# The front of a decoder block on one core, in two halves of the model width

## The chip, the cores and the metric

The kernel runs on one core of a Trainium2 chip. The metric is the device time of one execution in microseconds (us). Its engines are called TensorE (PE in the profile, its weight loads PEld), VectorE (DVE), ScalarE (ACT), GpSimd (POOL) and SyncE (SP, which here only issues DMAs). Each works through its own list of instructions in order and waits on semaphores for the others.

## What is computed

One layer with a sequence of 1024 tokens and model width 1024, in float32. The part that the change touches is its beginning:

```python
mod = (silu(c) @ w_ada + b_ada)[:, None, :]
sh1, sc1, g1, sh2, sc2, g2 = split(mod, 6)          # each of width 1024
h = rms_norm(x, norm1_g) * (1.0 + sc1) + sh1
proj = h @ w_in                                     # q 512 | k 128 | v 128 | u 512
```

After it come sliding-window attention over q, k, v (window 128, rotary positions, sinks), a pooling mixer over u, the projection with `w_o` gated by g1, and an MLP over h2 = RMSNorm(x) * (1 + sc2) + sh2, gated by g2.

## The kernel before

Tokens are handled in eight tiles of 128 (t = 0 to 7), the model width in eight chunks of 128 (k = 0 to 7, `KD` = 8, `P` = 128). Every engine's order is written out by hand.

**Loads.** SyncE walks the list `stream`. Its first 28 entries go round a ring of 12 buffers (four `raw`, eight `slots`): eight pieces of sh1's weights, eight of sc1's, four of `wu` (two chunks of the u weights each), eight of `wqkv` (one chunk of the q, k, v weights each). A piece of sh1 or sc1 holds one k row per partition and all 1024 columns, 512 KB. The load of entry n first waits (`freed`) until entry n - 12 has been used. x of tiles 0 and 1 is loaded behind the eighth entry (`load_x`); x of tile 2 behind the last of the 28, and it waits for the low half of h of tile 0 (`h_lo`), whose buffer it takes. The parameters and the next modulation pieces follow on the same queue.

**Modulation.** VectorE multiplies each piece with its column of `silu` and adds it (`add_piece`) into `acc` for sh1 and `acc_sc` for sc1, so that the sum over the partitions is still to be made. TensorE turns the 128x128 blocks of these sums (`turn_sums`), and VectorE reduces over the turned columns to `b1` (L1219) and to `a1` (`scale_1`, L1226), adds the bias from `cols` and, for `a1`, multiplies with norm1_g. `a1` and `b1` hold one scalar per model column.

**x.** ScalarE squares x (`square_x`), GpSimd makes the root (`root`, L1823 and L1825) behind the constants that it builds from the start (masks and pooling bands, L1767 to L1815), ScalarE scales (`scale_x`, L709), TensorE turns the tile (`turn_x`). VectorE (`make_h`, L1240) or ScalarE (`make_h_half`, L718) then makes h with `a1` and `b1`, a half of the model width at a time.

**High and low parts.** Products are made from numbers split in two: ScalarE copies the high part (`hi_h`, `hi_wu`, `hi_wqkv`), VectorE subtracts it to get the low part (`lo_h` L1246, `lo_wu` L1253, `lo_wqkv` L1259), and TensorE makes three products for each pair (`three`, L1969 to L1971), 512 columns wide for q and u and 256 for k and v. `project` loops over the eight chunks k into one PSUM bank.

**TensorE's order at the front.** Sums of sh1 turned; `keep_clock(8)`, which multiplies the identity with itself; x of tiles 0 and 1 turned; six more; the two halves of sc1's sums turned; `keep_clock(14)`; then u, q and kv of tile 0, u of tile 1, the pooling windows of tile 0 (`pool_windows`, L2095), x of tile 2 turned, q of tile 1, and so on.

The rows name lines; L1965 is the transpose helper `tr`, L1982 is `keep_clock`, L1166 the add of a piece and L1164 the first multiply, L1206 the two half-width adds of the last sc1 piece, L529 and L539 to L543 the loads of x and of the parameters.

Of the kernel before, what the change touches and what calls it, by code (L numbers as in the profile page):

```python
# [16 lines left out]
P = 128  # L17
# [36 lines left out]
def build(nc, x, c, positions, w_ada, b_ada, norm1_g, w_in, q_norm_g, k_norm_g, attn_sinks,  # L54
# [30 lines left out]
    with ExitStack() as ctx:  # L85
# [133 lines left out]
        stream = [("sh1", k) for k in range(KD)]  # L219
        stream += [("sc1", k) for k in range(KD)]  # L220
        stream += [("wu", k) for k in range(KD // 2)]
        stream += [("wqkv", k) for k in range(KD)]
# [11 lines left out]
        WO_POOL, WO_DVE = (0, 5, 6), (1, 2, 3, 4, 7)  # L234
        JOB_LOADS = (4, 4, 4, 3, 4, 4, 1, 0)
# [33 lines left out]
        sc1_turned = sem("sc1_turned")  # L269
# [56 lines left out]
        def rq(t):  # L326
            return rqs[:, NHD_ROOTS * (t % 3):NHD_ROOTS * (t % 3) + NHD_ROOTS]

# [139 lines left out]
        def freed(eng, n):  # L468
# [5 lines left out]
            if kind in ("sh1", "sc1"):  # L474

                eng.wait_ge(mod_summed, k + 1 + (KD if kind == "sc1" else 0) + (kind == "sc1" and k == KD - 1))
# [9 lines left out]
        def source(kind, k):  # L486
# [10 lines left out]
            m = mod_of[kind]  # L497
            return wada[:, k, m * D:(m + 1) * D]

        def target(kind, a):  # L500
            if kind == "wu":
# [18 lines left out]
        def _(sp):  # L520
# [5 lines left out]
            def load_x(t):  # L526
                if t >= 2:
                    sp.wait_ge(h_lo, 2 * (t - 1))
# [4 lines left out]
            for n in range(first_job):  # L533
                load(n)
                if n == 7:
# [155 lines left out]
        def _(act):  # L691
# [20 lines left out]
            def make_h_half(t):  # L712

                if t == 0:
                    act.wait_ge(a1_ready, 2)
                act.wait_ge(x_turned, t + 1)
                for k in range(NK, KD):
                    ins = nc.scalar.activation(xh[:, t % 2, k * P:(k + 1) * P], xT_banks(t)[:, k * P:(k + 1) * P],  # L718
                                               ACT.Identity, bias=b1[:, k:k + 1], scale=a1[:, k:k + 1])
                ins.then_inc(h_half[1], 1)  # L720
# [34 lines left out]
            hi_wqkv(6)  # L755
            hi_wqkv(7)
            hi_h(1, 1)
# [64 lines left out]
            def keep_u(t):  # L822
# [3 lines left out]
                nc.scalar.copy(usb[:, t % 2, :], bank(0)).then_inc(u_kept, 1)  # L826
# [322 lines left out]
        def _(dve):  # L1149
# [45 lines left out]
            for n in range(2 * KD):  # L1195
                if n >= 1:
                    dve.wait_ge(mod_summed, n)
                if n < KD:
                    add_piece(acc[:, :], ("sh1", n), n, mod_summed)
                elif n < 2 * KD - 1:  # L1200
                    add_piece(acc_sc, ("sc1", n - KD), n - KD, mod_summed)
                else:
                    a = landed(dve, ("sc1", KD - 1))
                    for h in range(2):
                        cut = slice(512 * h, 512 * h + 512)
                        v.scalar_tensor_tensor(out=acc_sc[:, cut], in0=a[:, cut], scalar=silu[:, KD - 1:KD],  # L1206
                                               in1=acc_sc[:, cut], op0=ALU.mult, op1=ALU.add).then_inc(mod_summed, 1)
                if n == 4:
                    dve.wait_ge(rows_in, 16 * 4)
                    v.tensor_copy(rows[64:72, :], posi[64:72, :]).then_inc(posf_ready, 1)  # L1210
                if n == KD + 2:

                    dve.wait_ge(rows_turned, 1)
                    v.tensor_copy(cols[:, :], psum[:, 4, 0:72]).then_inc(cols_ready, 1)
                if n == 2 * KD - 4:

                    dve.wait_ge(cols_ready, 1)
                    dve.wait_ge(mod_turned, 1)
# [1187 lines left out]
```

## Time and profile before

| what | value |
|---|---|
| median of 3 runs | 964.57 us (964.04 to 966.05) |
| profiled execution, its own time | 966.11 us |
| its span, first to last instruction | 964.4 us |
| granted TensorE clock, mean | 1.0 |
| TensorE busy | 925.0 us, 96% |
| VectorE busy | 657.4 us, 68% |
| ScalarE busy | 492.3 us, 51% |
| GpSimd busy | 352.6 us, 37% |

Times in the rows are counted from the start of the span of one profiled execution. The span lies 1.7 us below that execution's own time. A matmul's own duration overlaps with that of the next, so the pace of a series is read from start to start.

### The profile page before, as it was taken

The page shows a single profiled execution, that of the slowest core. Times are in us where ns is not written, and L with a number is a line of the kernel's source. Part 1 is how long each engine was busy: PE and PEld are TensorE (multiplying, and loading weights), DVE is VectorE, ACT ScalarE, POOL GpSimd, SP SyncE. Part 2 cuts the span into 40 slices and gives each one's busy share as a digit, 9 for nine tenths or more (in the row PEclk, how much of TensorE's full clock was granted, in tenths as well). Part 3 has the DMA queues.
Part 4 walks back from the last instruction along what each step waited for, and adds up shares of the span by engine and source line. Part 5 has one row for each costly group of instructions (what it writes and reads, how often), then busy time and mean ns, then how long its engine had stood idle before and what let it go on. Part 6 is the DMA issues. An engine that isn't in the chain of part 4 may idle for free.

```text
span 964.4 us, 12633 instructions
## 1 busy us (share of the span) xinstructions
PE 925.0 (96%) x4411; PEld 765.2 (79%) x4411; DVE 657.4 (68%) x1000; ACT 492.3 (51%) x874; POOL 352.6 (37%) x342
## 2 busy tenths in 40 slices
PE   1898999998999999999999999999999999999998
PEld 1787788886778888787888788888888888888887
DVE  6876887878644687665556544535786666779896
ACT  1656777778464564644554455454443444333331
POOL 8032222215232443988888877851000000000000
DMA  9852332214222240665456533538999637987673
GB/s 360 298 170 93 131 110 79 78 64 153 89 88 87 88 154 22 222 213 176 154 169 210 177 132 133 173 138 276 351 345 333 226 99 239 308 307 245 227 252 113
DMA packets 92271, 175.54 MB, mean 182 GB/s; under 512 B 9320, under 2 KB 26288, under 8 KB 92208
## 3 DMA queue, kind: packets, MB, share of 16 engines
q1 hardware_dynamic: 92096, 174.70, 53.1%
q8 instruction: 35, 0.57, 0.2%
q14 instruction: 28, 0.23, 0.1%
q10 hardware_dynamic: 112, 0.04, 0.0%
HBM read 136.95 MB, written 37.75 MB: 181 GB/s over the span
## 4 chain that ended last, share of the span: by engine, by line
PE 84%; DVE 6%; ACT 5%; POOL 3%; issue 2%; DVEq 0%; POOLq 0%; ACTq 0%
PE psum L1969 26%; PE psum L1971 25%; PE psum L1970 25%; PE psum L1965 3%; ACT probs L780 2%; PE psum L2045 1%; PE psum L2068 1%; ACT probs L788 1%; POOL band L1788 1%; PE psum L2095 1%; PE psum L2026 1%; PE psum L2023 1%; PE psum L2024 1%; ACT qT L799 1%; DVE probs L1297 1%
## 5 line engine op out<-in xcount | busy, mean ns | idle before, releaser
L1076 ACT CAST down_operands<-down_raw 128x1024 fp32r<-128x1024 f32 x96 | 100.9, 1054 | 153.4 <-PE psum L1971 58.1
L1969 PE MATMUL psum<-down_operands 128*128 128x512 f32 x448 | 174.3, 389 | 0.0
L1970 PE MATMUL psum<-down_operands 128*128 128x512 f32 x448 | 174.3, 389 | 0.0
L1971 PE MATMUL psum<-down_operands 128*128 128x512 f32 x448 | 174.3, 389 | 0.0
L1705 DVE TENSOR_TENSOR down_operands<-down_raw,down_operands 128x1024 fp32r<-128x1024 f32 x93 | 112.5, 1219 | 19.1 <-ACT down_operands L1076 18.5
L1969 PE MATMUL psum<-h2T,w_operands 128*128 128x512 f32 x272 | 107.5, 395 | 1.9 <-DVE act_quads_a L1649 1.3
L1971 PE MATMUL psum<-h2T,w_operands 128*128 128x512 f32 x272 | 105.9, 390 | 0.0
L1970 PE MATMUL psum<-h2T,w_operands 128*128 128x512 f32 x272 | 105.9, 389 | 0.0
L1921 POOL TENSOR_TENSOR w_operands<-raw,w_operands 128x512 fp32r<-128x512 f32 x56 | 83.2, 1487 | 42.1 <-ACT w_operands L1028 42.1
L1969 PEld LDWEIGHTS psum<-down_operands 128*128 128x128 f32 x448 | 84.1, 188 | 17.6
L1970 PEld LDWEIGHTS psum<-down_operands 128*128 128x128 f32 x448 | 84.1, 188 | 17.4
L1971 PEld LDWEIGHTS psum<-down_operands 128*128 128x128 f32 x448 | 84.1, 188 | 17.3
L1823 POOL TENSOR_SCALAR small<-small 128x1 f32<-128x1 f32 (+2 forms) x23 | 8.3, 359 | 169.1 <-DVE small L1366 131.7
L1971 PE MATMUL psum<-t_sums_hi,w_operands 128*128 128x512 f32 x168 | 65.4, 389 | 0.0
L1969 PE MATMUL psum<-t_sums_hi,w_operands 128*128 128x512 f32 x168 | 65.4, 389 | 0.0
L1970 PE MATMUL psum<-t_sums_lo,w_operands 128*128 128x512 f32 x168 | 65.4, 389 | 0.0
L1969 PE MATMUL psum<-w_in_hi,hT_hi 128*128 128x512 f32 (+1 forms) x168 | 61.7, 368 | 2.7 <-DVE hT_lo L1246 1.7
L1969 PEld LDWEIGHTS psum<-h2T,w_operands 128*128 128x128 f32 x272 | 51.1, 188 | 15.8 <-issue 3.8
L1921 POOL TENSOR_TENSOR w_operands<-w_sums,w_operands 128x512 fp32r<-128x512 f32 x42 | 55.9, 1343 | 11.8 <-ACT w_operands L1028 11.8
L1970 PEld LDWEIGHTS psum<-h2T,w_operands 128*128 128x128 f32 x272 | 51.1, 188 | 10.8 <-issue 0.5
L1971 PE MATMUL psum<-w_in_hi,hT_lo 128*128 128x512 f32 (+1 forms) x168 | 59.6, 355 | 0.0
L1971 PEld LDWEIGHTS psum<-h2T,w_operands 128*128 128x128 f32 x272 | 51.1, 188 | 10.7
(251 smaller groups left out, 1973.4 us busy)
## 6 DMA issues: line engine op xcount, KB each, us to landing
down_raw<-in_w_mlp_out SPq DMA_DIRECT2D x160, 256.0 KB, 4.3
down_raw<-act_scratch SPq DMA_DIRECT2D x112, 256.0 KB, 3.3
raw<-in_w_ada SPq DMA_DIRECT2D x32, 512.0 KB, 4.7
raw<-in_w_mlp_in SPq DMA_DIRECT2D x32, 512.0 KB, 4.9
act_scratch<-act_quads_a SPq DMA_DIRECT2D x64, 256.0 KB, 2.2
act_scratch<-act_quads_b SPq DMA_DIRECT2D x48, 256.0 KB, 3.6
slots<-in_w_ada SPq DMA_DIRECT2D x8, 512.0 KB, 10.5
xh<-in_x SPq DMA_DIRECT2D x8, 512.0 KB, 6.1
```

What stands on the lines that cost most here:

```text
L780: nc.scalar.activation(pr[:, kv, h, 0:w], pr[:, kv, h, 0:w], ACT.Exp, bias=negm[:, hh:hh + 1], scale=rq(i)[:, hh:hh + 1], accum_out=den[:, ...
L788: ins = nc.scalar.activation(pr[:, kv, h, 0:w], pr[:, kv, h, 0:w], ACT.Copy, scale=rden[:, kv * G + h:kv * G + h + 1])
L799: nc.scalar.copy(qT[r, :, :].rearrange("p (m e) q -> p m e q", e=2)[:, :, e, :], bank(1)[r, :].rearrange("p (m q) -> p m q", q=P))
L1076: nc.scalar.copy(o[:, 0, :, :], r[:, 0:2, :]).then_inc(op2_hi, 1)
L1297: ins = v.tensor_tensor_reduce(out=pr[:, kv, h, 0:w], in0=banks(4)[:, 256 * h:256 * h + w], in1=mask[:, m0:m0 + w], scale=1.0, scalar=-3e3 ...
L1705: v.tensor_tensor(o[:, 1, :, :], r[:, 0:2, :], f32(o[:, 0, :, :]), ALU.subtract).then_inc(op2_lo_dve, 1)
L1788: own_p.step(g.affine_select(out=cut, in_=cut, compare_op=ALU.is_ge, fill=0.0, base=base, pattern=[[1, n]], channel_multiplier=-1))
L1921: g.tensor_tensor(o[:, 1, :, :], quad, o[:, 0, :, :].bitcast(F32), ALU.subtract).then_inc(w1_lo, 1)
L1965: return nc.tensor.transpose(o, i, ident[0:rows_, 0:rows_])
L1969: mm(o, wh, ah, start=first, stop=False, skip_group_check=adds)
L1970: mm(o, wh, al, start=False, stop=False, skip_group_check=adds)
L1971: return mm(o, wl, ah, start=False, stop=last, skip_group_check=adds)
```

## The change

The two modulations sh1 and sc1 are made in two halves of 512 columns. A piece holds 512 columns of two k rows per partition (still 512 KB), and `stream` has sh1, sc1, wu and wqkv of the first half (4, 4, 2 and 4 pieces) and then those of the second. x of tiles 0 and 1 is loaded behind the fourth piece. VectorE adds each piece in two half-width instructions (`add_half`). Piece 4 of sh1 and of sc1 is not added by VectorE; TensorE multiplies it with `silu` straight into the column sums (`sum_piece`). The turning and reducing of the sums is replaced by matmuls with a column of ones (`sum_columns`, an output one column wide per block), and VectorE adds the bias from PSUM (`shift_1`, `scale_1`). The products of tile 0 and the u products of tile 1 are made for chunks 0 to 3 first and for chunks 4 to 7 later into the same banks (`project_half`); u of tile 1 has bank 4 to itself. h of tile 1 is made by ScalarE alone (`make_h_act`), h of tile 0 in its first half by VectorE and in its second by ScalarE. The first halves of h of both tiles come ahead of the second halves, which `h_count` counts. The sines of ScalarE move behind the pooled copy of tile 0, the root of x of tile 2 on GpSimd ahead of the root of q and k of tile 0. Counts of `mod_turned` and `mod_taken` drop by one throughout.

```diff
+        for h in range(2):
+            stream += [("sh1", 4 * h + j) for j in range(4)]
+            stream += [("sc1", 4 * h + j) for j in range(4)]
+            stream += [("wu", 2 * h + j) for j in range(2)]
+            stream += [("wqkv", 4 * h + j) for j in range(4)]
...
+        PE_PIECE = 4
...
+        def h_count(t, h):
+            return (2 * h + t if t < 2 else 2 * t + h) + 1
...
+            if kind in ("sh1", "sc1"):
+                at = m * D + 512 * (k // 4)
+                return wada[:, 2 * (k % 4):2 * (k % 4) + 2, at:at + 512]
...
                 if t >= 2:
-                    sp.wait_ge(h_lo, 2 * (t - 1))
+                    sp.wait_ge(h_lo, h_count(t - 2, 1))
...
-                if n == 7:
+                if n == 3:
                     load_x(0)
                     load_x(1)
```

ScalarE:

```diff
             hi_wu(0)
+            hi_h(0, 0)
             hi_wu(1)
-            hi_h(0, 0)
-            make_h_half(0)
-            hi_h(0, 1)
+            hi_wqkv(0)
+            hi_wqkv(1)
+            make_h_act(1, 0)
+            hi_h(1, 0)
+            hi_wqkv(2)
+            hi_wqkv(3)
             hi_wu(2)
             hi_wu(3)
-            for k in range(5):
-                hi_wqkv(k)
-            make_h_half(1)
+            hi_wqkv(4)
             hi_wqkv(5)
-            hi_h(1, 0)
+            for t in range(2):
+                make_h_act(t, 1)
+                hi_h(t, 1)
             hi_wqkv(6)
             hi_wqkv(7)
-            hi_h(1, 1)
...
-            sines()
             scale_x(2)
             keep_u(1)
             keep_pooled(0)
+            sines()
```

VectorE (the new list is whole from the first piece on):

```diff
+            def add_half(kind, k):
+                nonlocal summed
+                h, a = k // 4, landed(dve, (kind, k))
+                to = (acc if kind == "sh1" else acc_sc)[:, 512 * h:512 * h + 512]
+                for j in range(2):
+                    c_ = 2 * (k % 4) + j
+                    if summed >= 1:
+                        dve.wait_ge(mod_summed, summed)
+                    if j == 0 and k in (0, PE_PIECE + 1):
+                        v.tensor_scalar(to, a[:, 0:512], silu[:, c_:c_ + 1], None, ALU.mult).then_inc(mod_summed, 1)
+                    else:
+                        v.scalar_tensor_tensor(out=to, in0=a[:, 512 * j:512 * j + 512], scalar=silu[:, c_:c_ + 1],
+                                               in1=to, op0=ALU.mult, op1=ALU.add).then_inc(mod_summed, 1)
+                    summed += 1
...
+            for k in range(4):
+                add_half("sh1", k)
+            add_half("sc1", 0)
...
+            add_half("sc1", 1)
+            add_half("sc1", 2)
...
+            add_half("sc1", 3)
+            dve.wait_ge(cols_ready, 1)
+            shift_1(0)
             scale_1(0)
             make_h(0, 0)
-            scale_1(1)
             lo_wu(0)
             lo_h(0, 0)
             lo_wu(1)
+            lo_wqkv(0)
+            lo_wqkv(1)
+            lo_h(1, 0)
+            add_half("sh1", 5)
+            lo_wqkv(2)
+            lo_wqkv(3)
+            add_half("sh1", 6)
+            add_half("sh1", 7)
+            for k in range(PE_PIECE + 1, KD):
+                add_half("sc1", k)
+            lo_wu(2)
+            shift_1(1)
+            scale_1(1)
+            lo_wu(3)
             lo_h(0, 1)
-            lo_wu(2)
-            lo_wu(3)
-            for k in range(4):
-                lo_wqkv(k)
-            make_h(1, 0)
-            for k in range(4, KD):
-                lo_wqkv(k)
-            lo_h(1, 0)
+            lo_wqkv(4)
+            lo_wqkv(5)
             lo_h(1, 1)
+            lo_wqkv(6)
+            lo_wqkv(7)
```

TensorE (`column_sum` is one fp32 matmul with one moving column):

```diff
+            def sum_columns(at, sums, h):
+                for n in range(4 * h, 4 * h + 4):
+                    ins = column_sum(at, n, sums[:, n * P:(n + 1) * P], ones[:, 0:1], h == 0, True)
+                ins.then_inc(cols_summed, 1)
+            def sum_piece(at, kind):
+                a = landed(pe, (kind, PE_PIECE))
+                for j in range(2):
+                    for n in range(4):
+                        ins = column_sum(at, 4 + n, a[:, 512 * j + n * P:512 * j + (n + 1) * P], silu[:, j:j + 1],
+                                         j == 0 and n == 0, False)
+                ins.then_inc(piece_used, 1)
+            pe.wait_ge(mod_summed, 8)
+            sum_columns(1, acc, 0)
             pe.wait_ge(posf_ready, 1)
             tr(psum[:, 4, 0:72], rows[0:72, :], 72).then_inc(rows_turned, 1)
...
-            keep_clock(8, 2)
+            keep_clock(2, 2)
             turn_x(0)
             pe.wait_ge(cols_ready, 1)
             turn_x(1)
-            keep_clock(6, 2)
...
+            pe.wait_ge(mod_summed, 16)
+            sum_columns(2, acc_sc, 0)
             keep_clock(14, 0)
-            project_u(0)
-            project(bank(6), 0, AW, 0).then_inc(q_done, 1)
-            project(psum[:, 3, 0:2 * KVW], AW, QKV, 0).then_inc(kv_done, 1)
-            project_u(1)
+            project_half(bank(0), QKV, IN, 0, 0, u=True)
+            sum_piece(1, "sh1")
+            project_half(bank(6), 0, AW, 0, 0)
+            project_half(psum[:, 3, 0:2 * KVW], AW, QKV, 0, 0)
+            project_half(u_bank(1), QKV, IN, 1, 0, u=True)
+            pe.wait_ge(mod_summed, mod_count("sh1", KD - 1))
+            sum_columns(1, acc, 1)
+            sum_piece(2, "sc1")
+            pe.wait_ge(mod_summed, mod_count("sc1", KD - 1))
+            sum_columns(2, acc_sc, 1)
+            pe.wait_ge(b1_ready, 2)
+            keep_clock(12, 1)
+            project_half(bank(0), QKV, IN, 0, 1, u=True).then_inc(u_done, 1)
+            project_half(bank(6), 0, AW, 0, 1).then_inc(q_done, 1)
+            project_half(psum[:, 3, 0:2 * KVW], AW, QKV, 0, 1).then_inc(kv_done, 1)
+            project_half(u_bank(1), QKV, IN, 1, 1, u=True).then_inc(u_done, 1)
             pool_windows(0)
+            pe.wait_ge(u_kept, 2)
             turn_x(2)
```

## Rows read from the trace of the kernel before

**Rows 1.** The page: busy time, share of the span and instructions of each engine.

```profile
PE 925.0 (96%) x4411; PEld 765.2 (79%) x4411; DVE 657.4 (68%) x1000; ACT 492.3 (51%) x874; POOL 352.6 (37%) x342
```

**Rows 2.** Busy time by stretch: length, then each engine's, clock, DMA share, GB/s.

```profile
0.00:38.00 38.00, 15.56 (x90) 14.51 (x90) 27.91 (x38) 10.45 (x16) 22.28 (x70) 1.00 0.97 373
```

**Rows 3.** Timeline of TensorE: start, duration, what, count, idle before and its releaser.

```profile
22.38 3.78 PE L1982 MATMUL psum<-ident 128*128 128x128 f32 x16 [4.08 <-DVE squares L1166]
26.80 3.68 PE L1965 MATMUL psum<-ident,xh 128*128 128x128 f32 x16 [0.64 <-ACT xh L709]
...
32.94 3.29 PE L1982 MATMUL psum<-ident 128*128 128x128 f32 x28
37.97 0.50 PE L1969 MATMUL psum<-w_in_hi,hT_hi 128*128 128x512 f32 x1 [1.75 <-DVE hT_lo L1246]
...
51.00 0.28 PE L1969 MATMUL psum<-w_in_hi,hT_hi 128*128 128x256 f32 x1
...
53.86 0.40 PE L1969 MATMUL psum<-w_in_hi,hT_second 128*128 128x512 f32 x1
...
59.33 1.14 PE L2095 MATMUL psum<-band,u_rows 128*128 128x144 f32 x8
```

**Rows 4.** Timeline of VectorE, first piece to last low part.

```profile
5.21 0.75 DVE L1164 TENSOR_SCALAR acc<-raw,small 128x1024 f32<-128x1024 f32 x1 [1.07 <-DMA raw<-in_w_ada]
...
12.34 3.93 DVE L1166 SCALAR_TENSOR_TENSOR acc<-slots,small,acc 128x1024 f32<-128x1024 f32 x3
18.11 0.75 DVE L1164 TENSOR_SCALAR squares<-slots,small 128x1024 f32<-128x1024 f32 x1 [1.84 <-DMA slots<-in_w_ada]
...
24.89 1.22 DVE L1219 TENSOR_REDUCE small<-psum 128x8 f32<-128x1024 f32 x1
...
28.87 1.42 DVE L1206 SCALAR_TENSOR_TENSOR squares<-raw,small,squares 128x512 f32<-128x512 f32 x2
32.70 0.69 DVE L1226 TENSOR_REDUCE small<-psum 128x4 f32<-128x512 f32 x1 [2.42 <-PE psum L1965]
...
33.82 1.36 DVE L1240 TENSOR_SCALAR xh<-psum,small 128x128 f32<-128x128 f32 x4
...
36.09 1.22 DVE L1253 TENSOR_TENSOR w_in_lo<-slots,w_in_hi 128x1024 fp32r<-128x1024 f32 x1
37.23 0.68 DVE L1246 TENSOR_TENSOR hT_lo<-xh,hT_hi 128x512 fp32r<-128x512 f32 x1
...
46.60 3.55 DVE L1259 TENSOR_TENSOR w_in_lo<-raw,w_in_hi 128x768 fp32r<-128x768 f32 x4
```

**Rows 5.** Timeline of GpSimd in the first 26 us.

```profile
8.36 1.30 POOL L1796 TENSOR_TENSOR band<-band,ident 128x128 f32<-128x128 f32 x1
...
17.10 0.20 POOL L1791 TENSOR_SCALAR_AFFINE_SELECT band<-band 128x16 f32<-128x16 f32 x1
...
23.79 1.77 POOL L1825 TENSOR_TENSOR small<-small 128x2 f32<-128x2 f32 x1
```

**Rows 6.** Timeline of ScalarE from the scaling of x on.

```profile
25.59 2.19 ACT L709 ACTIVATE xh<-xh,small 128x1024 f32<-128x1024 f32 x2 [7.68 <-POOL small L1825]
28.74 1.05 ACT L733 CAST w_in_hi<-slots 128x1024 fp32r<-128x1024 f32 x1 [0.96 <-DMA slots<-in_w_in]
...
35.22 0.62 ACT L728 CAST hT_hi<-xh 128x512 fp32r<-128x512 f32 x1 [4.07 <-DVE xh L1240]
36.21 1.51 ACT L718 ACTIVATE xh<-psum,small 128x128 f32<-128x128 f32 x4 [0.37 <-DVE small L1231]
...
40.17 3.03 ACT L737 CAST w_in_hi<-slots 128x768 fp32r<-128x768 f32 x4
```

**Rows 7.** Timeline of SyncE's DMA issues: x of tile 2 and the last parameter.

```profile
39.68 0.33 SPq L529 DMA_DIRECT2D xh<-in_x  x1
...
42.59 0.43 SPq L543 DMA_DIRECT2D small<-in_attn_sinks  x1
```

**Rows 8.** DMA issues of the first 60 us: KB each, median us to landing.

```profile
small<-in_attn_sinks SPq DMA_DIRECT2D x1, 4.0 KB, 5.5
```

More of the change, by code:

```diff
@@ L215, in banks @@
             return psum[:, j:j + 2, :].rearrange("p b n -> p (b n)")
[L219 to L222, printed above, removed]
+        stream = []
+        for h in range(2):
[3 more added lines that the diff above has]
+            stream += [("wqkv", 4 * h + j) for j in range(4)]
         EARLY = len(stream)
@@ L234, in build @@
         WO_POOL, WO_DVE = (0, 5, 6), (1, 2, 3, 4, 7)
+        PE_PIECE = 4
+        DVE_PIECES = [(kind, 4 * h + j) for h in range(2) for kind in ("sh1", "sc1") for j in range(4) if 4 * h + j != PE_PIECE]
         JOB_LOADS = (4, 4, 4, 3, 4, 4, 1, 0)
@@ L474, in freed @@
             if kind in ("sh1", "sc1"):
-                eng.wait_ge(mod_summed, k + 1 + (KD if kind == "sc1" else 0) + (kind == "sc1" and k == KD - 1))
+                if k == PE_PIECE:
+                    eng.wait_ge(piece_used, 1 + (kind == "sc1"))
+                else:
+                    eng.wait_ge(mod_summed, mod_count(kind, k))
             elif kind in adaln_jobs:
@@ L497, in source @@
             m = mod_of[kind]
+            if kind in ("sh1", "sc1"):
+                at = m * D + 512 * (k // 4)
+                return wada[:, 2 * (k % 4):2 * (k % 4) + 2, at:at + 512]
             return wada[:, k, m * D:(m + 1) * D]
         def target(kind, a):
-            if kind == "wu":
+            if kind in ("wu", "sh1", "sc1"):
                 return a.rearrange("p (k n) -> p k n", k=2)
@@ L1193, in angles @@
                 v.tensor_scalar(a1_, a3, -1.0, float(np.pi / 2), ALU.mult, ALU.add).then_inc(angles_ready, 1)
[L1195 to L1218, printed above, removed]
-                    v.tensor_reduce(b1, banks(0).rearrange("p (k n) -> p k n", n=P), AX_X, ALU.add).then_inc(mod_taken, 1)
-                    dve.wait_ge(mod_taken, 1)
-                    own_d.step(v.tensor_tensor(b1, b1, cols[:, 8 * SH1:8 * SH1 + 8], ALU.add))
@@ L1988, in turn_sums, with project_half @@
                 return ins
-            def project(o, a, b, t, u=False):
-                for k in range(KD):
+            def project_half(o, a, b, t, half, u=False):
+                for k in range(4 * half, 4 * half + 4):
                     if u and k % 4 == 0:
-                        pe.wait_ge(h_lo, 2 * t + k // 4 + 1)
+                        pe.wait_ge(h_lo, h_count(t, half))
                     if t == 0 and u:
@@ L1999, in project @@
                     ins = three(o, h[:, k, :], l[:, k, :], wih[:, k, a:b], wil[:, k, a:b], k == 0, k == KD - 1)
+                return ins
+            def project(o, a, b, t, u=False):
+                for h in range(2):
+                    ins = project_half(o, a, b, t, h, u)
                 return ins
@@ L2101, in _, with column_sum @@
             pe.wait_ge(rows_in, 16 * 4)
+            def column_sum(at, n, a, by, first, last):
+                return mm(psum[:, at, n:n + 1], a, by, start=first, stop=last, skip_group_check=True)
+            def sum_columns(at, sums, h):
[11 more added lines that the diff above has]
+            sum_columns(1, acc, 0)
             pe.wait_ge(posf_ready, 1)
             tr(psum[:, 4, 0:72], rows[0:72, :], 72).then_inc(rows_turned, 1)
-            pe.wait_ge(mod_summed, KD)
-            turn_sums(banks(0), acc).then_inc(mod_turned, 1)
-            pe.wait_ge(mod_summed, 2 * KD - 5)
-            keep_clock(8, 2)
+            keep_clock(2, 2)
             turn_x(0)
```

73 lines of the change are left out of this document (41 added, 32 removed).

## The prediction

> **What bounds the kernel now.** The busy times come first: TensorE works 925.0 of 964.4 us [rows 1], so any time that is to be won lies where TensorE stands. The row of the first 38 us holds most of its 39 us of idle time: it works 15.56 us there, while the DMA engines are 0.97 busy at 373 GB/s [rows 2], and so 909.5 of the 926.4 us behind them. The front is the place. Its end I call the mark: the moment at which the products of tile 0 and the u products of tile 1 are done and the pooling windows start, 59.33 us [rows 3]. What TensorE does from the mark on is nearly the same list in both kernels, and nothing in it waits for an absolute time, so I take a shift of the mark as a shift of the end and look afterwards for what could eat it.
>
> Then the order of time on each engine. TensorE starts its first product at 37.97 us, released by VectorE's low part of h; 24 products of 512 columns take 59.33 - 53.86 = 5.47 us (0.228 each) and 24 of 256 columns 2.86 us (0.119 each) [rows 3]. VectorE is occupied from 5.21 us, when the first piece of the modulation has landed, to about 50.1 us, the end of its last low part of the q, k, v weights [rows 4]. The eleventh transfer (eight pieces and two tiles of x are ahead of or equal to it) is what VectorE waits for at 18.11 us, so one transfer of 512 KB costs (18.11 - 5.21)/10 = 1.29 us [rows 4]. TensorE still has some 9 us of products at 50.1 us. So before, VectorE's list sets the mark, and the transfers set only its first third.
>
> **Transfers.** The same bytes are loaded in another order. In 1.29 us steps the eight half-width pieces of the first half and the two tiles of x are there at 5.21 + 9 x 1.29 = 16.8 us, the last piece of the second half (eight more pieces, two of wu, four of wqkv at three quarters) at about 33.5 us, the last wqkv near 40 us. Rows of 2 KB instead of 4 KB could cost up to 5% by my estimate; 0.6 us at the first half, and it is covered in both halves, as follows.
>
> **First half on VectorE.** A full add is 3.93/3 = 1.31 us with its wait, a half one 1.42/2 = 0.71 without, 0.78 with it; the full first multiply is 0.75, a half one 0.48 by my estimate (half of what is over a fixed 0.2) [rows 4]. Four pieces of sh1 end at 11.1 us, VectorE waits for sc1 until 13.0, and the fourth sc1 piece is added by about 19.5 us. The reduces over turned sums (1.22 and twice 0.69 us [rows 4]) go; TensorE's column sums replace them.
>
> **What the first half then waits for.** In the changed list of TensorE the sums of sc1's columns stand behind both turns of x, and these stand behind the scaling of x, whose roots GpSimd makes after its constants. That root ends at 23.79 + 1.77 = 25.56 us before [rows 5], where it cost little. Now it is on the path. Does it come sooner? GpSimd's operation with SBUF inputs lasts 1.30 us beside VectorE's adds and a like small select 0.20 us while VectorE idles [rows 5]; each ends just after a VectorE instruction ends. With halves these ends come every 0.78 us. I went through GpSimd's 21 such operations from 5.3 us on: eight pass by 11.2 us, four in the gap to 13.0, seven by 19.4, and the last two (0.2 and 0.55 us) freely: the root is ready at 20.3 us. Bounds: 14.5 us if no operation were held up (they sum to 9 us), 25.6 us if nothing changes.
>
> From the root: ScalarE scales two tiles in 2.19 us [rows 6], TensorE starts 1.2 us after the first and turns both in 3.68 us [rows 3], so it is through at 25.2 us. Eight instructions with one column follow (an fp32 product is two). The trace shows none with one column. Not below 0.05 us each (half of a fast 128-column one, 3.29/28 = 0.117), not above 3.78/16 = 0.236, the slow 128-column one [rows 3]; I take 0.12, 1.0 us. With 0.2 of hand-over and two small VectorE operations (0.43 between the end of the second reduce and the first h, 33.39 to 33.82 [rows 4]) the first four scale columns are ready at about 27.0 us. VectorE has idled 7 us: that is the price of the change.
>
> **VectorE to the second half.** Its list: h of tile 0 1.36, low parts of two wu at 1.14, of four wqkv at 3.55/4 = 0.89, of two halves of h at 0.68, six pieces of modulation (two first multiplies, ten adds: 8.8 us), another wu 1.14 [rows 4]. That is 1.36 + 2.28 + 3.56 + 1.36 + 8.8 + 1.14 = 18.5 us, and 0.7 us of waiting for ScalarE, whose list from the first h (0.62 + 1.05 + 2 x 0.76 + 1.51 + 0.62 [rows 6]) ends as late. The sums end at 45.1, the wu at 46.2; TensorE's eight one-column instructions end at 46.2. The second scale columns are there at 46.8 us. ScalarE makes h (1.51) and its high part (0.62) [rows 6], VectorE the low part (0.68), with hand-overs 3.0 us: the second half of the products starts at 49.8 us. All transfers are over by then, and the loads are issued in time: the latest, of wqkv 4, is freed by a low part at about 37 us. The columns that VectorE saved (piece 4 of both, two reduces, h of tile 1) are 2 x 1.31 + 2.6 + 1.36 = 6.6 us; the idle 7 us and 0.14 us more for each of some dozen split adds eat them.
>
> **TensorE.** First half: free at 26.3 us, 28 instructions to hold the clock, then 12 products of u, eight column pairs, 12 and 12 of q and kv (held by the low parts until 37.5 us), 12 of u for tile 1, and the sums. This ends at about 44.8 us, just before VectorE's 45.1: little is spare. Second half: 36 x 0.228 + 12 x 0.119 = 9.6 us from 49.8 us; the low parts of wqkv come at 50.7, 51.5, 53.1, 54.0 us and are not late. The mark: **59.5 us, 0.2 later than before**.
>
> **Behind the mark.** x(2) and the parameters are issued when the low half of h for tile 0 is there: at 39.68 us before, the last of them at 42.59 [rows 7], with 5.5 us to landing [rows 8]. Now this is at 49.9 us, the last issue at 52.8, landing at 58.3 at the latest. VectorE's gain and sums of q, angles and h of tile 2 wait for it, up to 2.5 us later against the mark than before; TensorE's q of tile 1 needs the gain at mark + 1.8 and gets it at mark + 0.2. Were that cover gone, it would cost that same 2 us. The new wait of the third turn for the kept u is ended while the windows run (1.14 us); behind it stand only that turn and q of tile 1: 0.1 us. The sines move behind the pooled copy, and their user at mark + 11 us has room. Sum: +0.3 us.
>
> **Rivals.** (a) The clock, slower. TensorE's 128-column instructions went at 0.236 us from 22.38 until at least 30.5 us and at 0.117 from 32.94 on [rows 3]: the 1.2 and the 2.4 GHz level. The new list has a stretch of one-column instructions and waits from 42.6 to 46.2 us, ahead of the 24 that hold the clock. If the level falls there, these take 5.7 instead of 2.8 us, 2.2 more than the 3.5 us of h that cover them, and if the slow stretch lasts 8.1 us as the first one did, 2.4 us of the products run at half rate, which loses 1.2: the mark 3.6 later than before, 968.3 us. Against it: 1.7 us of idling ahead of 37.97 did no harm. It decides from a gap that lowers the level at all. (b) The first 28 holding instructions, which now follow 16 turned blocks and eight one-column instructions, all run slow, 6.6 us; TensorE starts its products at 33 us and is about 1.5 us late at the sums: 966.4 us. In my sum a good part of them is fast. For it: the 16 turns at 26.80 us ran at 0.23 us each though 16 holding instructions stood ahead of them [rows 3]. The Trainium skill (TensorE: Matmul & The Clock Gate, part on transposes) says that transposes do not count as work for the clock; the trace agrees as far as those 16 were slow, and by that rule (b) would be the outcome. (c) Faster: GpSimd's chain is held up less than I count; each microsecond off the root is one off the mark until TensorE's list, with its 0.3 us spare, is itself moved with it. A root at 17 us gives -3, 961.6 us. (d) VectorE is not the bound at all: then the last sc1 piece (33.5 us) sets the second half, behind wqkv 5 on ScalarE: products from 41.7 us, mark 51.4 us, 956.7 us. Its list speaks against it. (e) The change does nothing to the root: it stays at 25.6, everything 5.3 later, 970.2 us.
>
> **Numbers.** The profiled execution took 966.11 us with a span of 964.4; the median of the runs is 964.57. A shift of 0.3 us makes 964.9 us. What a measurement of this kernel can tell from no change is about 0.2%, 1.9 us. Chances: my sum within its own errors (one-column price -0.6 to +1.0 at two places, root 0.7, downstream 0.7) 0.38, range 963 to 966.7; (b) 0.10; (a) 0.20; (c) 0.19; (d) 0.06; (e) 0.07. Faster is (c) and (d), 0.25 in all; within 0.2% my sum and half of (b), 0.43; slower the rest, 0.32. The range from 960.5 to 969.3 us leaves out (d), (e) and tails.
>
> **What would show it.** Right: VectorE idle between about 19.5 and 26 us, ended by TensorE; GpSimd's root of the first tiles near 20.3 us; turns of x ending near 25.2; second-half products from about 50 us; windows at 59.5. Wrong: keep-clock instructions at 0.236 us behind 46 us; a root at 17 or 25; waits of TensorE for low parts of wqkv in the second half; VectorE waiting for the parameters so long that q of tile 1 waits too.

## The result and the profile after

The changed kernel takes 967.15 us (median of 16 runs, 966.01 to 968.56), the one before 964.84 (16 runs beside it, 964.04 to 966.52): 1.0022 times as long, 95% interval 1.0015 to 1.0028. The profiled execution has a span of 966.8 us (own time 968.56), 2.4 more than before. The page's busy row, and the stretch that answers to [rows 2] (length, each engine's busy time, clock, DMA share, GB/s):

```profile
PE 932.9 (96%) x4459; PEld 774.8 (80%) x4459; DVE 652.6 (68%) x1005; ACT 494.1 (51%) x878; POOL 349.6 (36%) x342
```

```profile
0.00:38.00 38.00, 20.12 (x104) 18.84 (x105) 24.00 (x41) 14.09 (x21) 16.53 (x70) 1.00 0.96 349
```

By 38 us TensorE has been busy 4.6 us longer than before, and the kernel is not faster: the work came sooner and its end did not. TensorE's timeline, which answers to [rows 3]:

```profile
21.04 3.67 PE L2006 MATMUL psum<-ident,xh 128*128 128x128 f32 x16 [4.12 <-ACT xh L731]
24.51 1.70 PE L2152 MATMUL psum<-ones,squares 128*128 128x1 f32 x8
26.08 5.23 PE L2023 MATMUL psum<-ident 128*128 128x128 f32 x28
31.07 0.48 PE L2010 MATMUL psum<-w_in_hi,hT_hi 128*128 128x512 f32 x1
33.88 1.84 PE L2152 MATMUL psum<-small,raw 128*128 128x1 f32 x16
...
43.44 1.93 PE L2152 MATMUL psum<-small,slots 128*128 128x1 f32 x16
45.23 1.03 PE L2152 MATMUL psum<-ones,squares 128*128 128x1 f32 x8
46.29 4.57 PE L2023 MATMUL psum<-ident 128*128 128x128 f32 x24
50.62 0.48 PE L2010 MATMUL psum<-w_in_hi,hT_hi 128*128 128x512 f32 x1
...
60.34 1.14 PE L2143 MATMUL psum<-band,u_rows 128*128 128x144 f32 x8
```

VectorE's and GpSimd's timelines, which answer to [rows 4] and [rows 5]:

```profile
5.39 0.49 DVE L1231 TENSOR_SCALAR acc<-raw,small 128x512 f32<-128x512 f32 x1 [1.99 <-DMA raw<-in_w_ada]
5.91 2.40 DVE L1233 SCALAR_TENSOR_TENSOR acc<-raw,small,acc 128x512 f32<-128x512 f32 x3
...
26.32 0.16 DVE L1249 TENSOR_TENSOR small<-psum,cols 128x4 f32<-128x4 f32 x1 [5.64 <-PE psum L2152]
...
40.99 4.04 DVE L1233 SCALAR_TENSOR_TENSOR squares<-slots,small,squares 128x512 f32<-128x512 f32 x5
...
46.56 0.16 DVE L1252 SCALAR_TENSOR_TENSOR small<-small,cols 128x4 f32<-128x4 f32 x1
...
48.95 0.69 DVE L1267 TENSOR_TENSOR hT_lo<-xh,hT_hi 128x512 fp32r<-128x512 f32 x1 [1.08 <-ACT hT_hi L749]
...
58.41 0.17 DVE L1432 TENSOR_SCALAR small<-small 128x8 f32<-128x8 f32 x1 [4.69 <-DMA small<-in_attn_sinks]
```

```profile
7.75 0.87 POOL L1838 TENSOR_TENSOR band<-band,ident 128x128 f32<-128x128 f32 x1
...
18.29 0.71 POOL L1865 TENSOR_SCALAR small<-small 128x2 f32<-128x2 f32 x1
19.09 0.72 POOL L1867 TENSOR_TENSOR small<-small 128x2 f32<-128x2 f32 x1
```

How to read them. The root is ready at 19.81 us, VectorE stands still for 5.64 us until the first scale columns come (26.32), its sums end at 45.03, and the low part of h for the second half is ready at 49.64. The row to stop at is TensorE's 46.29: 24 instructions that hold the clock in 4.57 us, 0.19 each, where the 28 of [rows 3] took 0.117 each. The first product behind them starts at 50.62, 0.98 us after h is ready. The windows by stretch (length, TensorE's busy time with its count, clock, DMA share, GB/s) say why, and show a second such place:

```profile
46.00:47.00 1.00, 0.96 (x9) 1.00 0.00 0
47.00:50.00 3.00, 3.00 (x17) 0.51 0.00 0
50.00:51.00 1.00, 1.00 (x8) 0.76 0.45 66
...
228.00:231.00 3.00, 3.00 (x8) 0.50 0.71 232
231.00:235.00 4.00, 4.00 (x24) 0.95 0.68 202
```

From 47 to about 50.4 us and from 228 to 231.3 us TensorE was granted 0.50, the 1.2 GHz level, while it was busy all the time. Before, no profiled stretch behind the start has that. (At the start of both kernels 128-column instructions go at 0.23 us each, the pace of the lower level, and yet the windows give 1.00 there; for the first 30 us the level is read from the pace.)

**Where the 2.4 us are.** The mark moves from 59.33 to 60.34 us, and the windows of tile 7 start at 221.30 instead of 220.22: 1.0 us from the front, nothing lost in the 160 us behind it. From the mark to the end of the span are 905.1 us before and 906.5 after. In ten of the twelve experiments below it is 904.9 to 905.5, and 906.3 in the other two: e9, which has the stretch at 228 us too, and e1, which has a wait behind the mark. So the rest, 1.3 us, is that stretch. TensorE waits 1.11 us there ahead of the pooling products and 0.72 ahead of the first products with w_o, but it does so in the kernel before and in e3 as well, where the level stays up. So the list of instructions and its waits do not bring it on by themselves.

Each run also gives its mean granted clock. A stretch of 3.4 us at half rate takes 3.4 x 0.5 / 965 = 0.002 off that mean. The kernel before had 1.0 in 23 of 28 runs of one batch. The changed one had it in none: 0.998, one stretch, in nine of 16 (median 966.79 us), 0.994 to 0.996 in seven (968.33). That is two such stretches or more, or one twice as long: the profile here has two with 0.996, and that of e7 below has one of 6.8 us with the same 0.996. The runs of the kernel before fall in two groups of their own, near 964.5 and 966.2 us, both at clock 1.0; its profile (966.11) is of the upper one. No profile of the lower one was taken, so what parts them stays open, and differences between profiles and between medians can differ by up to 1.7 us for that reason alone. One run of e8, 1176 us at a mean clock of 0.757, is left out below.

### The profile page after: what moved, and what is told of

Same layout as the page of the kernel before. It is cut to its first block, busy times and chain, and to the rows that moved or that the text cites. A ratio compares the mean times of both kernels' runs of the same rounds, so it can differ in the third digit from the quotient of the medians.

```text
span 966.8 us, 12740 instructions
## 1 busy us (share of the span) xinstructions
PE 932.9 (96%) x4459; PEld 774.8 (80%) x4459; DVE 652.6 (68%) x1005; ACT 494.1 (51%) x878; POOL 349.6 (36%) x342
## 4 chain that ended last, share of the span: by engine, by line
PE 86%; DVE 5%; ACT 5%; POOL 2%; issue 2%; DVEq 0%; POOLq 0%; ACTq 0%
PE psum L2010 26%; PE psum L2012 26%; PE psum L2011 26%; PE psum L2006 3%; ACT probs L804 2%; PE psum L2023 1%; PE psum L2093 1%; PE psum L2116 1%; ACT probs L812 1%; PE psum L2152 1%; PE psum L2143 1%; PE psum L2074 1%; PE psum L2072 1%; PE psum L2071 1%; ACT qT L823 1%
## 5 line engine op out<-in xcount | busy, mean ns | idle before, releaser
L1962 POOL TENSOR_TENSOR w_operands<-raw,w_operands 128x512 fp32r<-128x512 f32 x56 | 83.2, 1486 | 42.2 <-ACT w_operands L1052 42.2
```

Of the source, the lines that this page charges most:

```text
L1962: g.tensor_tensor(o[:, 1, :, :], quad, o[:, 0, :, :].bitcast(F32), ALU.subtract).then_inc(w1_lo, 1)
```

## The experiments

"Mark" is the start of the pooling windows; since the first load lands between 4.9 and 5.5 us in different profiles, the second number is the mark less VectorE's first piece. Even so it is not exact: in the seven profiles whose lists are the same up to the first scale columns (changed, e1, e3, e5, e7, e8, e9) these columns come 19.50 to 20.93 us behind the first piece, and the changed kernel's profile is the latest. So a difference of a microsecond in the mark says nothing unless rows show where it arises. Ratios are to the kernel before on the same chip (whose medians there were 964.65 to 966.18, since they fall in one or the other of its two groups); they are not quotients of two medians.

| kernel | mark / from first piece | slow stretch in the front | span | median, ratio (95%) |
|---|---|---|---|---|
| before | 59.33 / 54.12 | none | 964.4 | 964.84 |
| changed | 60.34 / 54.95 | 47 to 50.4 | 966.8 | 967.15, 1.0022 (1.0015 to 1.0028) |
| e1_sums_earlier | 58.71 / 53.60 | 34.7 to 38.2 | 965.0 | 970.05, 1.0045 (1.0030 to 1.0059) |
| e2_root_earlier | 56.69 / 51.21 | 40.6 to 47.4 | 961.8 | 963.59, 0.9985 (0.9977 to 0.9994) |
| e3_less_adds | 58.29 / 52.99 | 45.0 to 48.4 | 963.8 | 965.95, 1.0012 (1.0001 to 1.0022) |
| e5_no_hold | 60.83 / 55.61 | 46.5 to 53.3 | 966.1 | 967.49, 1.0022 (1.0013 to 1.0031) |
| e7_params_first | 59.87 / 54.81 | 43.6 to 50.4 | 964.9 | 966.91, 1.0019 (1.0010 to 1.0028) |
| e8_sums_params | 61.71 / 56.26 | 35.4 to 42.2 | 966.7 | 968.9, 1.0035 (1.0022 to 1.0049) |
| e9_spread_params | 60.18 / 54.80 | 46.6 to 50.0 | 966.5 | 966.05, 1.0006 (0.9997 to 1.0015) |
| e10_root_spread_params | 56.20 / 51.00 | none | 961.3 | 963.03, 0.9970 (0.9958 to 0.9982) |
| e4_root_earlier_old | 56.97 / 51.82 | none | 962.0 | 963.83, 0.9990 (0.9981 to 0.9998) |
| e11_short_hold | 55.77 / 50.46 | 23.4 to 30.2 | 960.7 | 962.73, 0.9974 (0.9963 to 0.9984) |
| e12_old_colsums | 59.26 / 54.38 | none | 964.3 | 966.04, 1.0011 (1.0000 to 1.0023) |
| e13_old_root_colsums | 55.41 / 50.33 | none | 960.5 | 962.92, 0.9973 (0.9964 to 0.9982) |

### The terms of the changed kernel

**The one-column instructions of sc1 moved away from the holding series.**

```diff
             sum_piece(1, "sh1")
+            sum_piece(2, "sc1")
...
             sum_columns(1, acc, 1)
-            sum_piece(2, "sc1")
```

> The 16 one-column products of sc1's fourth piece move ahead of q of tile 0, so that one-column work ahead of the second holding series is 1.9 us instead of 3.7. Theory (the clock falls because of the one-column stretch, and the slow holding series is what moved the mark): the 24 holding instructions take 2.8 us instead of 4.57, the second half starts at 49.7 instead of 50.62, the windows at 59.4 instead of 60.34; the whole about 1 us below the changed kernel, 966.2. Rival (the level falls at a moment of its own, whatever stands there): the slow stretch stays near 47 us and the windows at 60.3.

TensorE's timeline and windows of it:

```profile
31.56 1.84 PE L2152 MATMUL psum<-small,raw 128*128 128x1 f32 x16
33.26 2.21 PE L2152 MATMUL psum<-small,slots 128*128 128x1 f32 x16
...
45.39 2.92 PE L2023 MATMUL psum<-ident 128*128 128x128 f32 x24
48.96 0.50 PE L2010 MATMUL psum<-w_in_hi,hT_hi 128*128 128x512 f32 x1 [0.65 <-DVE hT_lo L1267]
...
79.29 1.16 PE L2116 MATMUL psum<-pooledT,pool_w 128*128 128x128 f32 x8 [1.34 <-DVE pooledT L1390]
```

```profile
35.00:38.00 3.00, 3.00 (x9) 0.50 1.04 386
```

The holding series is fast again (2.92 us) and TensorE now waits 0.65 us for h, so the 0.98 us were the clock's. The slow stretch did not go: it begins at 34.7 us in the last of the joined 32 one-column instructions and slows the products of q behind them instead. Of the 1.35 us by which the mark is nearer to the first piece, 0.88 was there already at the first scale columns, ahead of the edit. It came out slower: 970.05 us, and the row of 79.29 shows a new wait of 1.34 us behind the mark. Its profile was its lowest run (966.77, clock 0.998); the five others, at 0.993 to 0.995, had more of such stretches, at places that no profile shows.

**The root ahead of the last pooling band.** `root` of x of tiles 0 and 1 is moved on GpSimd ahead of the constants of the last window.

```diff
             for i, w in enumerate(POOL_WINDOWS):
+                if i == 3:
+                    pool.wait_ge(x_squared, 2)
+                    root(rx[:, 0:2], ssx[:, 0:2], D, x_root)
```

> GpSimd makes the root of x of tiles 0 and 1 ahead of its last pooling band. Theory (the root is on the path of the changed kernel): scaling starts at 15.4 us instead of 19.84, the sums of sc1's columns end at 22 instead of 26.2, VectorE's idle time in front of them falls from 5.6 to about 1.5 us, the windows start 2 to 3.9 us earlier (56.4 to 58.3; the smaller gain if TensorE's holding series stays at the slow level), the whole 963 to 965. Rival (TensorE's or the transfers' time sets the second half): the windows move by less than 0.5 us.

ScalarE's timeline:

```profile
14.60 2.19 ACT L731 ACTIVATE xh<-xh,small 128x1024 f32<-128x1024 f32 x2 [1.31 <-POOL small L1840]
```

The scaling of x starts 5.2 us earlier, VectorE's wait for the first scale columns falls from 5.64 to 1.18 us, the mark comes 3.65 earlier, and the span ends 5.0 earlier (1.3 of it the stretch at 228 us, which its profile lacks). A late root was what the first half paid for. The holding series was wholly slow here, 5.47 us, and the products start 1.60 us after h is ready (44.88 and 46.48), which eats part of the gain.

**Fewer columns to add.** The four adds of sc1's pieces 6 and 7 cover 8 columns instead of 512, so those products are left out of the scale.

```diff
-                        v.scalar_tensor_tensor(out=to, in0=a[:, 512 * j:512 * j + 512], scalar=silu[:, c_:c_ + 1],
-                                               in1=to, op0=ALU.mult, op1=ALU.add).then_inc(mod_summed, 1)
+                        n = 8 if kind == "sc1" and k in (6, 7) else 512
+                        v.scalar_tensor_tensor(out=to[:, 0:n], in0=a[:, 512 * j:512 * j + n], scalar=silu[:, c_:c_ + 1],
+                                               in1=to[:, 0:n], op0=ALU.mult, op1=ALU.add).then_inc(mod_summed, 1)
```

> The four adds of sc1's pieces 6 and 7 cover 8 columns instead of 512 (the modulation is not whole then). Theory (VectorE alone sets the second half): its sums are ready 2.2 us earlier, 42.9 instead of 45.0, and the windows start 2.2 us earlier. Rival (TensorE's own list ends at the same time, 45.2 us, as the sum had it with 0.3 us to spare): the windows move by 0.2 to 0.5 us only, and TensorE shows no waiting ahead of the last sums.

The mark comes 1.96 earlier from the first piece. One microsecond of that was there already at the first scale columns, which the edit does not touch; the medians, of different batches, differ by 1.2. VectorE then waits (its row stands below the two of TensorE):

```profile
43.37 1.03 PE L2153 MATMUL psum<-ones,squares 128*128 128x1 f32 x8
44.26 4.55 PE L2024 MATMUL psum<-ident 128*128 128x128 f32 x24
```

```profile
44.51 0.16 DVE L1250 TENSOR_TENSOR small<-psum,cols 128x4 f32<-128x4 f32 x1 [1.48 <-PE psum L2153]
```

So VectorE's adds are worth about 1 us and then TensorE's list sets the second half: the two end together, as the prediction had it.

**No holding series before the second half.** `keep_clock(12, 1)` is taken out.

> The 24 holding instructions ahead of the second half are left out; the function is the same. Theory (TensorE waits for their slow end, h is ready earlier): the second half starts at 49.7 instead of 50.62, but at the slow level for some 3 to 4 us, so that 512 columns take 0.43 to 0.46 us; the windows at 61 to 61.5, 0.7 to 1 later. Rival (the level does not depend on them): fast products from 49.7, windows at 59.4, 1 us earlier.

TensorE waits idle for h instead, the clock is low from 46.5 to 53.3 us, and the first 512-column products are 0.43 us apart instead of 0.23:

```profile
49.12 0.77 PE L2010 MATMUL psum<-w_in_hi,hT_hi 128*128 128x512 f32 x1 [3.48 <-DVE hT_lo L1267]
49.69 0.63 PE L2011 MATMUL psum<-w_in_lo,hT_hi 128*128 128x512 f32 x1
```

The mark is 0.66 later, the median 0.3, within its spread; since the first scale columns came 0.53 sooner here, from them the loss is 1.2. To delay TensorE by 1 us or to run its first products slowly costs nearly the same.

**The parameters ahead of x of tile 2**, alone, with e1's move, and with `sum_piece(2, "sc1")` placed behind kv of the first half instead:

```diff
-            load_x(2)
...
             sp.dma_start(sink, attn_sinks.to_broadcast([P, NH])).then_inc(params_in, 16)
+            load_x(2)
```

> The changed kernel with SyncE issuing the five parameter loads ahead of x of tile 2, so that they no longer wait for h. Theory (behind the mark VectorE's list from the parameters on has no time to spare): VectorE's wait of 4.69 us for the sinks goes, its gain of q starts near 56.5 instead of 59.31 us; the windows of tile 0 stay at about 60.3; the whole is the same as the changed kernel in an execution where TensorE had no wait (967), or up to 1 us less where it had one. Rival (the parameters cost nothing anywhere): no difference in any row of TensorE behind the mark.

> The parameter loads first, and the one-column products of sc1's fourth piece ahead of q of tile 0, as in the run that had the windows at 58.71 but took 970. Theory (what that run won at the mark it lost to the late parameters, 1.34 us of waiting ahead of the second pooling products in its profile): the windows of tiles 1 and 2 are 18.7 us apart instead of 19.96, and the median falls to 964 to 965. Rival (the slow stretch of the clock that it has at 34.8 us, or more of them, makes the 970): the median stays above 968.

> The parameter loads first, and the one-column products of sc1's fourth piece between kv of tile 0 and u of tile 1, so that no two groups of 16 stand together and the holding series follows 16 one-column instructions instead of 32. Theory (long one-column stretches lower the clock): no slow stretch between 31 and 60 us, holding instructions 2.8 us, windows at 59.3; the median 964 to 965. Rival (the level falls anyway): a slow stretch of 3.4 us is found somewhere between 31 and 51 us and the median is that of the run with the parameters first alone.

e7 gains nothing over the changed kernel (1.0019 beside 1.0022): the late parameters are hidden there. With e1's move they are not: tiles 1 and 2 start their windows 19.96 us apart in e1 and 18.72 in e8, so the wait of e1 is theirs, 1.2 to 1.3 us. e8 still takes 968.9 us, as its rival had it: behind the mark it loses nothing (905.0 us), but its mark is the latest of all, with 6.8 us at half rate from within the one-column instructions on, with TensorE never idle:

```profile
36.00:41.00 5.00, 5.00 (x17) 0.50 0.91 295
```

e9, whose one-column work stands in three groups of 16 instead of 16 and 32, had a mean clock of 1.0 in one run (964.60 us), 0.998 in nine (median 966.05) and 0.996 in one (968.21, the profiled one, slow again at 228 us). That is some 1.5 to 2 us a stretch, from single runs at both ends. Its theory missed and its rival held: shorter groups did not keep the level up, and the holding series was as slow as in the changed kernel:

```profile
46.12 4.57 PE L2023 MATMUL psum<-ident 128*128 128x128 f32 x24 [0.16 <-DVE small L1241]
```

### Is it the halves?

**Early root with e9's order.**

> All three: GpSimd's root of x ahead of its last pooling band, the one-column products spread, the parameters first. Theory (the three costs are separate): 3.5 us less than the run with the latter two, windows at 55.5 to 56.5, median 961 to 962, faster than the kernel before by 0.3%. Rival (TensorE's list becomes the bound of the second half): no more than the 963.59 of the root alone.

```profile
42.83 2.92 PE L2023 MATMUL psum<-ident 128*128 128x128 f32 x24
```

The front has no slow stretch behind its start, and VectorE waits for TensorE's sums (0.35 and 0.80 us). TensorE's list is that of e9, where the level fell; only the times differ. So the grouping of the one-column work does not decide it, and what does is open. 0.9970 is faster than both kernels of the study.

**The same with `keep_clock(4, 0)` for `keep_clock(14, 0)`.**

> The run with all three edits, and the first holding series cut from 28 to 8 instructions. Theory (in that run TensorE's list was 1.1 to 1.3 us late at the sums because of a slow holding series of 6.30 us): the first products start at 25 instead of 27.66 us, partly at the slow level, the last sums follow VectorE's last add at once, the windows move from 56.20 to 55.0 to 55.5; median 962 to 962.5. Rival (without the series the products themselves run slow for as long): the windows stay or move later by up to 1 us.

```profile
24.87 0.80 PE L2010 MATMUL psum<-w_in_hi,hT_hi 128*128 128x512 f32 x1 [2.66 <-DVE hT_lo L1267]
```

Products start at 24.87 instead of 27.66 us and the mark moves by 0.4 only (0.9974). That is the rival: TensorE idles 2.66 us, the granted clock is 0.50 from 23.4 to 30.2 us, and the first 12 products take 5.3 us where e10's took 2.9, so that the next instructions start at 30.16 instead of 30.58. VectorE still waits for TensorE's sums, 0.55 and 0.80 us. What TensorE would be worth if it were faster there is not shown.

**The early root in the kernel before.**

> The kernel before with GpSimd's root of x of tiles 0 and 1 ahead of its last pooling band, as in the run of the changed kernel that gained 3.6 us. Theory (before the change the root had time to spare, VectorE's adds set the first scale columns): scaling starts 5 us earlier (20.5 instead of 25.59), the windows stay within 0.3 us of 59.33, no difference in the time. Rival (the root mattered before, too): the windows move by more than 1 us.

This is where my theory fell. I held that the late root cost that kernel little, and its mark moves by 2.3 us. The median moves by 0.8 only (964.65 to 963.83): the profile before is of the slower of its two groups, and how much of the 2.3 the faster one has to give was not measured. The timelines of ScalarE and VectorE, beside [rows 6] and [rows 4]:

```profile
19.61 2.19 ACT L709 ACTIVATE xh<-xh,small 128x1024 f32<-128x1024 f32 x2 [1.57 <-POOL small L1798]
```

```profile
30.31 0.69 DVE L1226 TENSOR_REDUCE small<-psum 128x4 f32<-128x512 f32 x1
```

The reduce that stood at 32.70 us behind a wait of 2.42 stands at 30.31 with none. TensorE had been late with the turned sums because they were queued behind the turns of x, and these behind the root.

**Column sums without halves.** In the kernel before, both `turn_sums` become one-column matmuls and the three reduces go.

```diff
-                own_d.step(v.tensor_reduce(a1[:, c4], bank(2 + h).rearrange("p (k n) -> p k n", n=P), AX_X, ALU.add))
...
+                own_d.step(v.tensor_tensor(a1[:, c4], psum[:, 2 + h, 0:4],
...
+            def sum_columns(o, sums):
+                for n in range(o.shape[1]):
+                    ins = mm(o[:, n:n + 1], sums[:, n * P:(n + 1) * P], ones[:, 0:1], start=True, stop=True)
```

> The kernel before, whole width, with one part of the change alone: one-column products in place of the turned sums and VectorE's three reduces. Theory (VectorE's list set the mark, and the reduces are 2.6 us of it; the halves were not needed for this): b1's reduce of 1.22 us becomes 0.17, the two of 0.69 go, eight one-column instructions take 0.9 to 1.9 us for four turned blocks at 0.5: the windows at 57.2 to 57.8 instead of 59.33, median 962.8 to 963.4. Rival (sc1's last pieces or the clock take their place): less than 0.7 us.

> The kernel before, whole width, with the root early and the one-column sums. Each alone moved the windows by -2.3 (root) and by nothing (sums, with VectorE waiting 4.85 us for TensorE). Theory (the late root hid what the sums save on VectorE): with both, VectorE's last add ends at 28.9 us and its 4.85 us of waiting shrink to about 1, the windows start at 54.5 to 55.5, median 961.5 to 962.5; the halves of the change are then not needed for the gain, the best halved kernel having its windows at 55.77 and a median of 962.73. Rival (the transfers or the weights set the time by then): the windows stay at 56.5 or later, and the halved kernel is ahead.

Alone it brought nothing (1.0011): VectorE's adds end 1.4 us sooner, at 28.89, and its wait for TensorE is 4.85 us where it was 2.42. But the profile is not a clean test of the sums. Its root came later as well, 26.70 us instead of 25.56, since a copy of GpSimd at 21.03 us was held for 1.16 us (0.18 before), ahead of the first reduce that the edit takes out. The first columns came 1.0 us later with it. With the root at its old time the edit might have brought about that microsecond, by my estimate from these two times; no run shows it. The clock counts against e12 too: six of its 12 runs have a mean of 0.998 or less, two of 25 of the kernel before beside it. ScalarE's scaling behind the late root, then the same row of VectorE in e12 and with both edits:

```profile
26.73 2.19 ACT L709 ACTIVATE xh<-xh,small 128x1024 f32<-128x1024 f32 x2 [8.87 <-POOL small L1822]
```

```profile
33.74 0.16 DVE L1225 TENSOR_TENSOR small<-psum,cols 128x4 f32<-128x4 f32 x1 [4.85 <-PE psum L2106]
```

```profile
29.90 0.16 DVE L1225 TENSOR_TENSOR small<-psum,cols 128x4 f32<-128x4 f32 x1 [0.83 <-PE psum L2106]
...
55.41 1.14 PE L2092 MATMUL psum<-band,u_rows 128*128 128x144 f32 x8
```

With the root early as well the mark is at 55.41 us and the ratio 0.9973. The whole change with the same early root (e2, 0.9985), and with three more edits besides (e11, 0.9974), is no better: in none of these kernels do the halves of the model width bring anything beyond the two small edits.

## Why the prediction was right, and where not

**Right, point by point.** Root at 20.3 us (19.8), VectorE idle from 19.5 to 26 (20.7 to 26.3), turns through at 25.2 (24.7), VectorE's sums at 45.1 (45.0), second scale at 46.8 (46.7), low part of h at 49.8 (49.6), parameters at 58.3 (58.4) and hidden (e7). The mechanism was as said: the idle time in the first half eats what VectorE saves. Part of the agreement is luck, though. The root came 0.5 us early, and the eight one-column instructions behind it took 1.70 us instead of 1.0, as they went at the slow pace. The pieces of sc1 were there at 14.0 us, not at 13.0, which the late root covered. And other profiles with the same list have the first scale columns up to 1.4 us sooner. That GpSimd's chain runs faster behind half-width adds held in size: its held operations last 0.71 to 0.87 us beside them. The Trainium skill (SBUF — State Buffer, part on who interferes with whom) says that a VectorE instruction with two inputs in SBUF contends with a GpSimd one that reads SBUF, and that the ports they share are locked exclusively; the trace agrees as far as the duration on GpSimd went down with the length of VectorE's adds, 1.30 to 0.72 us with 1.31 to 0.80.

**Mis-sized term: the second holding series.** I counted 24 x 0.119 = 2.8 us, hidden behind h; it took 4.57 and put the products 0.98 us late. That is rival (a) at less than a third of its price (0.98 of 2.2 + 1.2 = 3.4 us): the clock fell, but it fell after the series had begun, and by 50.4 us it was back, so the products themselves were hardly slowed. That the one-column stretch ahead of it was the reason, as (a) had it, is not shown. The sum of the prediction was a mark at 59.5; its own terms, 0.16 us early at h, plus 0.98 give the 60.34 measured.

**Rival (b)** did not come. The first 28 holding instructions took 5.23 us, partly slow, where (b) had 6.6 and my sum a good part fast; in e1 they took 3.37, all at the fast pace, behind 16 turned blocks and eight one-column instructions of 1.33 us. In e7 the pace rose before the turned blocks were through, 16 in 3.30 us instead of 3.67. So the turned blocks did not keep the level down in these runs as the rule cited for (b) would have it. Of the profiled kernels only e10 had the series slow as a whole, 6.30 us. TensorE's reserve at the sums was gone all the same: they ended at 45.23 us, not 44.8, just behind VectorE's 45.03.

**A term not in the sum: the clock elsewhere.** By its mean clock every run of the changed kernel has at least one slow stretch, and seven of 16 have twice as much slow time or more, at 1.5 us in the median. The profile shows a second stretch at 228 us, in the first products with w_o, worth 1.3 us. Two profiles of 13 changed or edited kernels have it, both of kernels with halves. What brings it on is open.

**A wrong reading: "where it cost little".** The prediction named VectorE's list as what sets the mark before, and so put the root off the path. It was on it: the 2.42 us in [rows 4], released by TensorE, lead through [rows 3] (turns at 26.80, behind 0.64 us of ScalarE) and [rows 6] (7.68 us for GpSimd) to [rows 5]. e4 shows it by taking the late root away, and in e12 the first columns moved with the root, a microsecond later. It did not touch the forecast, since the sum for the new kernel was built from the root on; it would have told beforehand that work saved ahead of the first scale columns could not pay while the root was late.

**The size.** 964.9 was forecast, 967.15 came. That is inside 960.5 to 969.3, but outside the 963 to 966.7 us that my own sum had with its errors, and it got inside the wide range only through the room left for the rivals. The ratio of 1.0022 lies at the bound between no difference and slower: +0.2 of the profile's 1.0 us at the mark was forecast, the clock took the rest of it, and the 1.3 us behind the mark were in no term.

## What to carry to other kernels

When an engine's work is cut and its end doesn't move, follow the wait that took its place back through every queue to the first engine that was late: here two scalars of GpSimd, queued behind constants that nobody needed yet, were worth 0.1% by themselves and more than a rebuilt front, which was worth nothing. Before work is split to start it sooner, move the late input first, alone, and see what is left to win. And look at the granted clock wherever a series takes longer than the same series elsewhere: rearranging TensorE's list moved such stretches about, and no edit here was shown to prevent them.

## What the runs showed of the hardware

- A one-column fp32 matmul costs as much as one of 128 columns: 16 in 1.84 us (0.115 each) at 33.88 us of the changed kernel, eight in 1.70 (0.21) at 24.51, where everything still goes at the slow pace; [rows 3] have 0.117 and 0.236 for 128 columns.
- The granted clock can fall to 0.50, the 1.2 GHz level, with TensorE busy throughout: at 47 us in the changed kernel, 34.7 in e1 and 35.4 in e8, in or just behind one-column instructions. That these are the reason is not shown: e9 and e10 have the same list on TensorE, and it fell in e9 and not in e10; at 228 us it fell in products 512 columns wide in the changed kernel and in the wait ahead of them in e9, and other profiles have the same products and waits without a fall.
- Of GpSimd's 21 operations with SBUF inputs ahead of the root's end, those beside VectorE's adds ended one by one as these did. In the changed kernel, with adds half as long and the pauses between them at other times, the root is ready at 19.81 us instead of 25.56, with GpSimd's own list up to it unchanged.
